# First pair of three stages as eight plain products of four weight quarters, and part 0's input normalised in two halves

## The reference

```python
a = rmsnorm(x, g_mix);  u = a @ w_in          # q, k, v, gates, o, B, C, h
h = mlstm_chunkwise(q, k, v, ...)             # four heads, plus a short convolution of C * h
x = x + concat(sigmoid(o) * headnorm(h), B * conv(C * h)) @ w_out
f = rmsnorm(x, g_ffn)
x = x + (silu(f @ w_gate) * (f @ w_up)) @ w_down
e = rmsnorm(pe @ w_ple, g_ple)
x = x + sigmoid(x @ w_pg) * e
y = rmsnorm(x, g_final)
```

## Time and profile before

| | |
|---|---|
| time, median of 3 | 2670.49 us (2669.78 to 2672.49) |
| profiled execution | 2669.71 us, of which the span is 2668.0 us |
| granted TensorE clock, mean | 0.976 |
| PE / PEld busy | 2504.5 us (94%) / 2441.3 us (92%) |
| DVE (VectorE) busy | 1477.2 us (55%) |
| ACT (ScalarE) / POOL (GpSimd) busy | 906.4 us (34%) / 1043.4 us (39%) |
| HBM traffic | 378.9 MB read, 126.3 MB written, 189 GB/s |

### The profile page before, as it was taken

One profiled execution on the slowest core, in us unless ns is written; L12 is line 12 of the kernel. 1 busy time (PEld: TensorE's weight loads), 2 busy tenths in 40 slices (PEclk: granted clock), 3 DMA queues, 4 the chain that ended last, 5 costly groups with the idle time before them and its releaser, 6 DMA issues.

```text
span 2668.0 us, 41317 instructions
## 1 busy us (share of the span) xinstructions
PE 2504.5 (94%) x15882; PEld 2441.3 (92%) x15882; DVE 1477.2 (55%) x2291; ACT 906.4 (34%) x1691; POOL 1043.4 (39%) x863
## 2 busy tenths in 40 slices
PE   4899798999999989999999999998999999999997
PEld 3899687999999989999999999998899999999997
DVE  4666787765565574466643333477347664333355
ACT  4335353433333533333421112343234432212233
POOL 3566655666676332322331222323322323222233
PEclk6999898999999999999999999999999999999998
DMA  5555644666576656566456455575557555554544
GB/s 166 194 185 189 229 167 166 221 223 227 206 252 231 209 157 212 167 228 197 158 182 206 149 169 171 175 220 186 183 177 234 181 199 167 197 193 163 174 144 158
DMA packets 292392, 507.86 MB, mean 190 GB/s; under 512 B 23892, under 2 KB 188037, under 8 KB 291687
## 3 DMA queue, kind: packets, MB, share of 16 engines
q1 hardware_dynamic: 211846, 272.28, 30.3%
q10 hardware_dynamic: 80352, 232.94, 26.8%
HBM read 378.89 MB, written 126.27 MB: 189 GB/s over the span
## 4 chain that ended last, share of the span: by engine, by line
PE 68%; DVE 9%; DMA 5%; issue 3%; POOL 2%; ACT 1%; DVEq 0%; POOLq 0%; SPq 0%; ACTq 0%
PE bank L547 22%; PE bank L549 21%; PE bank L548 21%; DMA wring<-weight_parts 3%; POOL wring L2498 2%; DMA weight_parts<-wring 1%; DVE qlo L1645 1%; PE bank L647 1%; DVE sg L2357 1%; DVE ess L2229 1%; PE bank L658 1%; DMA wraw<-w_gate 0%; PE bank L710 0%; DMA xs<-x_prompt 0%; PE bank L637 0%
## 5 line engine op out<-in xcount | busy, mean ns | idle before, releaser
L547 PE MATMUL bank<-qhi,wring 128*128 128x352 f32 (+1 forms) x3588 | 1176.9, 328 | 104.6 <-issue 20.1
L2498 POOL TENSOR_TENSOR wring<-wraw,wring 128x512 fp32r<-128x512 f32 x528 | 769.7, 1467 | 1278.5 <-ACT wring L1179 1275.9
L549 PE MATMUL bank<-qhi,wring 128*128 128x352 f32 (+1 forms) x3588 | 1159.1, 323 | 0.0
L548 PE MATMUL bank<-qlo,wring 128*128 128x352 f32 (+1 forms) x3588 | 1158.0, 323 | 0.0
L547 PEld LDWEIGHTS bank<-qhi,wring 128*128 128x128 f32 x3588 | 685.9, 191 | 132.8 <-issue 115.2
L548 PEld LDWEIGHTS bank<-qlo,wring 128*128 128x128 f32 x3588 | 685.7, 191 | 0.0
L549 PEld LDWEIGHTS bank<-qhi,wring 128*128 128x128 f32 x3588 | 683.6, 191 | 0.0
L1179 ACT ACTIVATE wring<-wraw 128x512 fp32r<-128x512 f32 x528 | 329.4, 628 | 755.0 <-PE bank L549 593.9
L547 PE MATMUL bank<-hid,wring 128*128 128x352 f32 (+1 forms) x1056 | 340.7, 323 | 11.8 <-DVE wide L2316 7.1
L549 PE MATMUL bank<-hid,wring 128*128 128x352 f32 (+1 forms) x1056 | 339.2, 321 | 0.0
L548 PE MATMUL bank<-hid,wring 128*128 128x352 f32 (+1 forms) x1056 | 338.2, 320 | 0.0
(11 more groups left out here) (305 smaller groups left out, 2441.7 us busy)
## 6 DMA issues: line engine op xcount, KB each, us to landing
wring<-weight_parts ACTq DMA_DIRECT2D x428, 512.0 KB, 4.5
weight_parts<-wring SPq DMA_DIRECT2D x206, 512.0 KB, 3.8
wraw<-w_down SPq DMA_DIRECT2D x33, 1024.0 KB, 7.1
wraw<-w_in SPq DMA_DIRECT2D x12, 1024.0 KB, 6.9
wraw<-w_in SPq DMA_DIRECT2D x48, 256.0 KB, 4.4
wraw<-w_gate SPq DMA_DIRECT2D x11, 1024.0 KB, 6.5
wraw<-w_up SPq DMA_DIRECT2D x11, 1024.0 KB, 6.2
wraw<-w_gate SPq DMA_DIRECT2D x44, 256.0 KB, 3.5
```

What stands on the lines that cost most here:

```text
L547: nc.tensor.matmul(o, hi, mh, start=begins, stop=False, skip_group_check=True)
L548: nc.tensor.matmul(o, hi, ml, start=False, stop=False, skip_group_check=True)
L549: return nc.tensor.matmul(o, lo, mh, start=False, stop=ends, skip_group_check=True)
L2498: nc.gpsimd.tensor_tensor(wlo[e % RING][:, :].rearrange(v, k=k), w.src, whi[e % RING][:, :].rearrange(v, k=k), ALU.subtract).then_inc(lo_d ...
```

## The change

It does four things.

- **Plain pairs.** `in` 0, `out` 0 and `gate` 0 no longer use the seven-product scheme. Their four weight quarters are each multiplied twice, in the order A11·B11, A21·B11, A12·B21, A22·B21, A11·B12, A21·B12, A12·B22, A22·B22, and two products add up in one of four banks. No weight sums are made, kept or loaded for these pairs, and all three parts load 1 MB raw. B12 becomes an operand of its own (number 7, in the slot of operand 6). `in` corners are copied out by ScalarE, `gate` corners by ScalarE with Silu, `out` corners added by VectorE. `gates(q)` takes four groups instead of five. The duos are gone: `out` 1 is a pair in five banks, `up` 0 a pair in three.
- **Order of operands.** T1, T2 and the rest are made during the plain pair; in parts 0 and 1 the normalising for the next part begins at product 12 of `pg` instead of 16, and T3 and T4 move from the end of `pg` into the next `in` stage.
- **Part 0's head.** Squares, roots, spreading and normalising go by halves (three tiles each); `R` is no longer normalised in place but into `wide`; stores of x move from ScalarE's queue to SP's; gains are loaded as 40 rows of 512 bytes and transposed on TensorE; ScalarE starts with a dummy Square as soon as `epst` is set; `AHEAD` work is spread among the steps.
- **Residual roots.** Column sums behind k == 4, the two spreads behind k == 7 and k == 8. The outputs of the part before (`y_gained`) move from products 6, 10, ... 26 to 7, 11, 15, 19, 23, 26 of `in`.

```diff
+PLAIN_PAIRS = {("in", 0): (0, 1, 2, 6), ("out", 0): (0, 1, 2, 3), ("gate", 0): (0, 1, 2, 6)}
+PLAIN_ENTRIES = ("A11", "A21", "A12", "A22")
+PLAIN_PRODUCTS = (("a", 0, 0, 0), ("b", 1, 0, 1), ("P2", 2, 1, 0), ("P4", 3, 1, 1),
+                  ("c", 0, B12, 2), ("d", 1, B12, 3), ("P3", 2, 2, 2), ("P5", 3, 2, 3))
+PLAIN_AHEADS = (0, 5, 6, 7)
...
-                for b, terms in enumerate((((0, 0), (1, 1)), ((0, 0), (0, 4), (1, 2)))):
+                for b, terms in enumerate((((0, 0), (1, 1)), ((0, B12), (1, 2)))):
...
-                    if k == 6:
+                    if k == 4:
                         pe.wait_ge(res_sum, 8 * (q.n + 1))
                         column_sums(("res", q.n), q, 5, ss)
-                    if k == 9:
-                        pe.wait_ge(res_root, 2 * (q.n + 1))
-                        for b in range(2):
-                            spread(("res", q.n, b), q, b, 3 + b, mean_roots)
+                    if k in (7, 8):
+                        pe.wait_ge(res_root, 2 * q.n + k - 6)
+                        spread(("res", q.n, k - 7), q, k - 7, 3 + k - 7, mean_roots)
... TensorE, head of part 0 and in_after
+            for t in range(3):
+                first_features(t)
+            gain_columns()
+            x_spread(supers[0], 0)
+            first_features(3)
+            first_features(4)
+                    if not q.n and s == 0:
+                        first_features(5)
+                    if not q.n and s == 1:
+                        x_spread(q, 1)
... ScalarE, head of part 0
+            link(nc.scalar.activation(junk[:, 0:1], epst[:, 0:1], ACT.Square))
+            for t in range(3):
+                first_squares(t)
+            act.wait_ge(consts_made, 1)
+            ahead()
+            high_of(q, "in", 0)
+            first_squares(3)
+            x_evict(q, 3, X_BANKS[3][0], 0)
+            ahead()
+            first_squares(4)
+            x_evict(q, 4, X_BANKS[4][0], 0)
+            high_of(q, "in", 1)
+            first_squares(5)
+            x_evict(q, 5, X_BANKS[5][0], 0)
+            ahead()
+            ahead()
+            high_of(q, "in", B12)
+            high_of(q, "in", 2)
... ScalarE, gate 0
+            def gate_evict(q):
+                def evict(c, b, bk):
+                    if (c, b) == (0, 0):
+                        act.wait_ge(low, LOW[(q.n, "ffn", 4)])
+                    nc.scalar.activation(sl[:, c, q.blocks[b]], bank[bk][:, 0:q.N], ACT.Silu).then_inc(silu_done, 1)
... VectorE, part 0's head
+            for t in range(3):
+                for m in range(2):
+                    x_evict(q, t, m)
+            gains()
             in_part(q, "B11")
+            in_part(q, "B21")
+            low_of(q, "in", 0)
... VectorE, pg of the part before
-                    for at_, part in ((16, "B11"), (17, "T1"), (18, "B21"), (19, "B22"), (20, "T2"), (23, "T3")):
+                    for at_, part in ((12, "B11"), (13, "B21"), (17, "B12"), (18, "B22"), (25, "T1"), (27, "T2")):
...
-                if q.n < 2:
-                    nxt = supers[q.n + 1]
-                    in_part(nxt, "T4")
-                    for i in (6, 3):
-                        low_of(nxt, "in", i)
                 gated_add(q, 3, 1)
                 gated_add(q, 3, 0)
... GpSimd
-                pool.wait_ge(x_sq, NTILE * (q.n + 1))
-                for a, z, n in ((0, 5, P), (5, 6, q.tiles[5][1])):
+                pool.wait_ge(x_sq, NTILE * q.n + (3, 6)[half])
+                for a, z, n in (((0, 3, P),), ((3, 5, P), (5, 6, q.tiles[5][1])))[half]:
... SP queue
             for t in range(NTILE):
                 sp.dma_start(xin[t][0:q.tiles[t][1], :], x_source(q, t)).then_inc(xin_in[t], 16)
                 if t == 2:
+                    gains_rows()
                     raw()
+            first_x_stores((0, 1, 2))
+            constants()
             raw()
-            constants()
+            first_x_stores((3, 4, 5))
```

More of the change, by code:

```diff
@@ L359, in add_pairs @@
[L359 to L364 removed]
+            turn = {n: n_sums[0] + j + 1 for j, n in enumerate(turns)}
+            n_sums[0] += 4
+            shift = [sum(1 for k in spares if k < j) for j in range(len(names))]
+            where = {n: e0 + j + shift[j] for j, n in enumerate(names)}
+            for j, n in zip((0, 1, 3, 6), turns):
+                sums_at.setdefault(e0 + j + shift[j], []).append((n, r, at_, where, turn))
@@ new lines, in add_pair @@
+        for j, n in enumerate(names):
+            if n in views:
+                add_entry(r, views[n], turn.get(n, 0), n == first)
+                if not stored and (n in turn or n == "A11"):
+                    keep_entry(of, n)
+                end[r] = n_prepared[0]
+            else:
+                n_loads[0] += 1
+                entries.append(Entry(r, None, 0, False, None, None, kept_as[(of, n)]))
+                entries[-1].loads = n_loads[0]
+            if j in spares:
+                add_spare(r, spares[j])
@@ L585, in pair, with plain_pair @@
                     after(base + j)
-            def duo(q, one, two, after):
-                for j, name in enumerate(FIRST_PRODUCTS):
-                    product(q, *one, name)
-                    after(2 * j)
-                    product(q, *two, name)
-                    after(2 * j + 1)
+            def plain_pair(q, st, i, after, base):
+                banks, stage, e = banks_of(st, i), st if st in STAGES else "ffn", n_entry[0]
+                for j, (name, n, op, corner) in enumerate(PLAIN_PRODUCTS):
+                    bk, starts = banks[corner], j in (0, 1, 4, 5)
+                    hi = whi[(e + n) % RING][:, :].rearrange("p (k n) -> p k n", k=4)
+                    lo = wlo[(e + n) % RING][:, :].rearrange("p (k n) -> p k n", k=4)
+                    entry_ready(e + n)
+                    operand_ready(q, stage, op)
+                    if starts:
+                        take(bk)
+                    for k in range(4):
+                        last = three(bank[bk][:, 0:q.N], hi[:, k, :], lo[:, k, :], qhi[:, slot(op), k, 0:q.N],
+                                     qlo[:, slot(op), k, 0:q.N], starts and k == 0, not starts and k == 3)
+                    multiplied((q.n, st, i, name), bk, last)
+                    operand_end[(q.n, stage, op)] = entry_end[e + n] = n_prod[0]
+                    if j < 7:
+                        after(base + j)
+                n_entry[0] += 4
             def gates(q):
@@ L951, in _ @@
-                for p in range(1 if DUO_FFN else 0, FFP):
+                plain_pair(q, "gate", 0, ffn_after(q), 0)
+                pair(q, "up", 0, ffn_after(q), 7)
+                for p in range(1, FFP):
                     pair(q, "gate", p, ffn_after(q), 14 * p)
@@ L1547, in _ @@
-                for p in range(1 if DUO_FFN else 0, FFP):
+                high_of(q, "ffn", B12)
+                plain_pair(q, "gate", 0, gate_evict(q), first_gate_after(q), 0)
+                pair(q, "up", 0, None, up_after(q, 0), 0)
+                for p in range(1, FFP):
                     pair(q, "gate", p, sl[:, 0, q.blocks[0]], gate_after(q, p), 0, ACT.Silu)
@@ L2633, in pair, with plain_pair @@
                     after(base + j)
+            def plain_pair(after):
+                for j in range(8):
+                    if j in PLAIN_AHEADS:
+                        ahead()
+                    if j < 7:
+                        after(j)
             def nothing(s):
```

745 lines of the change are left out of this document (331 added, 414 removed).

## The result

| | before | after |
|---|---|---|
| time, median of 5 | 2670.49 us (2667.13 to 2672.49) | 2685.83 us (2679.52 to 2688.12) |
| span of the profiled execution | 2668.0 us | 2684.1 us |
| ratio | | 1.0054, 95% interval 1.0039 to 1.0070 |

The changed kernel is half a per cent slower. Forecast were 2606 us and a range of 2585 to 2650: the forecast was wrong in sign, and by 80 us.

What follows compares the result with a forecast made beforehand. PE, busy 94% of the span, was taken as the bound; +11.4 - 28.4 - 17.0 - 12.4 - 17.2 - 2.6 - 0.5 + 2.0 = -64.7 us against 2669.7 gave 2605.0, forecast as 2606, range 2585 to 2650.

Steps and rivals of the forecast that it cites:

- The extra work: Plain pairs of out and gate, three parts: 72 more matmuls, +11.4 us, all on PE's path; in costs nothing.
- Head of part 0: Start of part 0, worked by halves: pair 1 of in starts at 53.2 instead of 81.6 us, saving 28.4.
- Rival 2: Head's halves don't run apart, so it saves 13 instead of 28.4 us: 2620 us; chance 12%.
- Gates wait for their second weight entry: Last step of part 0's head: ScalarE prepares the entry by 45.5 us, then four groups take 7.6 us.
- `pg` into `in`: Both part changes: earlier normalising, T3 and T4 leaving the end of pg give -10.2 and -7.0 us.
- y outputs: y_gained in in, one product before PE wants its banks: +1 us in each of parts 1 and 2.
- Entries of `out` and `gate`, part 0: Fewer weight sums on VectorE: -17.0 us at out, 6 remaining; -12.4 at gate, 16 remaining.
- Entries in parts 1 and 2: Out and gate entries: -2.6 us together at out, -0.5 at gate; bounds +8 to -6 for all four.
- rival 3: PE waits at plain pairs of parts 1 and 2, 8.8 us at four entries: slower, 2688 us; chance 6%.
- Rival 1: VectorE stays the bound at the entries and only the head gains: 2655 us; chance 17%.
- The rule on the port: VectorE and GpSimd share ports, the loser blocks: qlo 2.72 instead of 1.62 us beside GpSimd's weight entries.
- The three signs of a wrong forecast: Head saves under 20 us; PE waits over 3 us on GpSimd's operand-2 qlo per plain pair; VectorE's qlo mean above 2.

Runs made afterwards that it cites:

- g2: f3 with T4 subtracted one product sooner, ahead of the low half of T2 on VectorE: 2642.8 us, ratio 0.9905.
- h2: g2 with gate_bias ahead of the low half of T3 on VectorE: 2633.3 us, ratio 0.9873.
- e3: The changed kernel with GpSimd's clear_parts behind product 8 of in instead of 4: 2677.9 us, ratio 1.0035.
- f3: f2 with GpSimd's clear_parts after product 8 instead of 4, as in e3: 2652.9 us, ratio 0.9950.
- f4: f3 with five gate groups and ScalarE's high half of T3 ahead of its two weight conversions: 2651.8 us, ratio 0.9941.
- f1: The changed kernel with the y tiles put back toward their old places on VectorE and gate_logs after product 11 instead of 10: 2674.9 us, ratio 1.0026.
- f2: f1 with pair 1's product P4 in bank 0 instead of bank 7: 2660.7 us, ratio 0.9976.
- g1: f3 with the low half of operand 2 at the out and gate entries made by VectorE instead of GpSimd: 2660.8 us, ratio 0.9961.
- e1_bank: The changed kernel with pair 1's last product of in in bank 0 instead of bank 7: 2685.6 us, ratio 1.0071.
- e4_all_three: The changed kernel with the edits of e1_bank and e3 and five gate groups together: 2675.2 us, ratio 1.0033.
- i1: f4 with T4 sooner as in g2 and gate_bias ahead of T3's low half as in h2: 2638.9 us, ratio 0.9892.

## Why the prediction was wrong

**The extra work** was right: PE has the 72 matmuls more, and the steps of the `out` and `gate` entries in parts 1 and 2, once T4 comes sooner (g2, h2), are +0.7 to +2.4 us each, around the product of 1.9.

**Head of part 0.** Its steps held until the gates. The changed kernel's PE timeline of the head:

```profile
10.91 0.91 PE L667 MATMUL bank<-ident,x_roots 128*128 128x128 f32 x6 [0.21 <-POOL x_roots L2530]
...
17.86 0.63 PE L546 MATMUL bank<-qhi,wring 128*128 128x352 f32 x1 [2.01 <-issue]
...
25.23 1.29 PE L667 MATMUL bank<-ident,x_roots 128*128 128x32 f32 x8 [0.92 <-POOL x_roots L2530]
26.46 0.43 PE L546 MATMUL bank<-qhi,wring 128*128 128x352 f32 x1
```

The first product starts at 17.86 (18.8 forecast), the second spread is done as the third product starts, at 26.46 (28.5 and 29), and the eighth ends at 43.97 (43). Rival 2 is out. The step that failed is the last one, "Gates wait for their second weight entry, which ScalarE prepares ...: 45.5". They began at 52.14, after 8.17 us, and the first of them ran at the slow clock. I had asked only when ScalarE prepares the entry (45.64 us, so that time was right), not what stands behind that: GpSimd's part of the entry, with 3.35 us of clearing ahead of it that waits for a low half of VectorE, and the bank that ScalarE has to copy out first. So pair 1 starts at 61.3 instead of 53.2. The clearing ended last, but the 8 us don't hang on it alone: without it (e3, f3) pair 1 starts at 61.95 and 61.96, because the copy of bank 6 ends next. T4 sooner (g2) brings 59.28, h2 58.39. The last 5 us of this miss stay open.

**`pg` into `in`.** T3 and T4 no longer stand at the end of `pg`, and the first product of `in` comes 4.6 and 3.3 us sooner against the last pair of `pg`. PE's wait on `gated_add` (L2359 before, L2382 after) fell from 2.4 to 1.0 us. But the wait on VectorE's combining of the last pair only moved: from 3.1 and 2.9 us ahead of the last product of `pg` to 1.7 and 1.6 there and 3.6 and 3.5 ahead of the second product of `in`. From 911 to 955 us of the changed kernel:

```profile
PE bank L546 <- DVE sg L1712: 5.3, 2, 3.6
PE bank L656 <- DVE wide L2382: 1.0, 1, 1.0
```

The larger part was lost at the gates, to GpSimd's clearing and the late T4: the forecast was -10.2 and -7.0, measured were -2.0 and +1.9; without the clearing (e3) they are -4.5 and -2.7, with T4 sooner as well (g2) -6.2 and -4.2. I had said "the plain pair wants T1 to T4 only for pair 1, 22.8 us later" and did not follow T3 to where it lands: it shares its slot with B12, so it can't be written before the gates end, at which time pair 1 begins. Room of 22.8 us was room of zero. By itself that is worth little over 1 us a part (f4); it counts through what stands behind T3 on VectorE. With the order mended (h2) the two stretches give -7.1 and -3.0, at or inside the bounds of the forecast.

**y outputs.** This is the step that failed most: "+1 us in each of parts 1 and 2". I measured the move by one product, and left out what it was moved past: the low half of T3, `gate_bias` and, for the second tile, `gate_logs`, each with a wait of its own. It was the question that costing a moved step should have asked. Pair 1 lost 12.6 and 12.4 us, and 5.3 in part 0, where there are no y tiles and bank and gate chain alone are at work. f1 and f2 show it: with the order of the y tiles and the bank put back, the step of pair 1 falls by 9.5 and 9.3 us. The whole kernel gains 25 us between the profiled spans (2684.1 and 2658.8), 21 by the ratios. `gate_bias` ahead of the low half of T3 (h2) takes another 1.2 and 1.1 us, and 4.0 in part 0.

The Trainium skill, "PSUM — Partial Sum Buffer", Engine vs sequencer instructions, says of the queues of ScalarE, VectorE and GpSimd that they are strictly first in, first out; the rows of 955 to 1005 us agree: VectorE spent 13.87 us ahead of T3 while the first tile of y, whose root GpSimd had made by 958.80, stood behind it, and ScalarE 13.37 us ahead of T3's high half.

**Entries of `out` and `gate`, part 0.** Forecast -15.1 and -10.5, measured -5.0 and -1.1, and -7.2 and -3.8 in h2. The mechanism was there (the waits of the earlier trace rows on L1755 are gone), the size was not. I let 6 and 16 us remain by counting VectorE's work; what remains, 15.2 and 25.5, is waits of other classes and the slow clock beside them.

At `out` the gain lies ahead of its first product, 8.4 us, where the wait of 6.1 us on L1705 went. From there to the embedding the changed kernel takes 3.4 us more, the extra product included: its longest wait comes at 309.25 us. PE's waits from 266 to 312 us:

```profile
PE bank L546 <- DVE t L1715: 4.3, 1, 4.3
PE bank L546 <- DVE u L1715: 2.9, 1, 2.9
...
```

VectorE was busy without a wait from 302.39 to 309.10 us, and 3.37 us of that are sums of the residual's squares (L2184, L2187), which now stand ahead of the combining that PE waits for; my count of VectorE's work at this entry left them out. That they set the wait is read from the order, not tried.

At `gate`, the changed kernel's waits of PE from 343 to 439 us:

```profile
PE bank L546 <- POOL wring L2508: 4.6, 1, 4.6
PE bank L546 <- DVE u L1739: 4.4, 2, 3.8
PE bank L546 <- DVE wide L2339: 3.9, 1, 3.9
PE bank L546 <- POOL qlo L2522: 2.6, 1, 2.6
...
```

The 3.8 is the one of the earlier trace rows that I had said would stay. The 4.6 on GpSimd is 0.7 in h2_bias_first, whose entry is 2.7 us shorter; the other three stay (5.1, 4.5 and 2.6). What sets them was not tried. This part of the miss, some 10 us at each of the two entries, is located but its cause stays open.

**Entries in parts 1 and 2.** Forecast +4.5 in all with the extra products, measured +13.7, within the bound (8 + 7.6) but at its far end. The new wait of P3 on GpSimd was named but taken, with that of T3, at half a us; it was 1.9 us at the `gate` entry of part 1, and 1.7 to 1.9 are left in g2 and h2. The T4 chain was not seen; g2 shows it to be worth 10 us over all parts, half of that in `in`.

**The rivals.** The time fell beside rival 3's 2688, but not by rival 3: its four entries lost 13.7 us together and not 35, and the loss lay in pair 1 of `in`. Rival 1 had the right kind of cause. VectorE isn't full at pair 1 of `in`, though: its queue waits. The rule on the port holds where the two engines meet. f3_outputs_bank0_late at the entry of `out`, VectorE and GpSimd, and then g1_low2_vector's VectorE, where GpSimd makes no low half:

```profile
1167.76 4.65 DVE L1869 TENSOR_TENSOR wide<-wide 128x1408 f32<-128x1408 f32 x1
```

```profile
1167.68 3.24 POOL L2523 TENSOR_TENSOR qlo<-wide,qhi 128x1408 fp32r<-128x1408 f32 x1 [1.88 <-ACT qhi L1227]
```

```profile
1168.10 1.62 DVE L1874 TENSOR_TENSOR wide<-wide 128x1408 f32<-128x1408 f32 x1
```

T1 takes 1.62 us alone. With GpSimd's 3.24 beside it, begun 0.08 us earlier, it takes 4.65 and ends 1.49 us after GpSimd's, as though it had begun only then. The Trainium skill, "SBUF — State Buffer", Terms, has this rule, and the trace agrees. But over all of VectorE's low halves the mean didn't rise (1785 ns before, 1773 after; by source both ways, from `qraw` 1823 to 1782, from `mixq` 1605 to 1925). And g1, which takes GpSimd's low half away at these entries, gains 1 us at each `out` entry of parts 1 and 2 and loses 3 at each `gate` entry. So the rule doesn't carry the loss, as rival 1 would have it.

The three signs of a wrong forecast hardly spoke. The head saved 20.3 us, just over the 20. PE's wait on GpSimd's low half was over 3 us in one plain pair alone (`in` of part 0, 3.3). And VectorE's low halves, from 8 us ahead of a plain pair to the next pair, took 1.55 to 1.81 us in the mean in parts 1 and 2; only `in` and `gate` of part 0 were above 2 (2.11 and 2.16; 1.62 and 2.05 before). None of them looked at pair 1 of `in`, where most was lost.

## What to carry to other kernels

A step that is moved in a hand-written order is to be priced by the waits that it now stands behind on its engine, and by who wants its result, not by how far it moved: here one place in VectorE's queue, with a bank that was given back late as well, was worth 9 us in each of two parts. An operand that gets room in time needs room in memory as well: look up which buffer it shares and who reads that last. And where two waits stand one behind the other, taking away one can show nothing (e1_bank, e4_all_three); look how long the others grew before a suspect is dropped, and take them away together. A wait that ended last also isn't worth its length: e3 took 4.7 us of PE's wait away in the head, and pair 1 came no sooner.

## What the runs showed of the hardware that was not expected

- The clock can make a stall dearer than its length, and the same stall doesn't always do it. In f1_outputs_first the gate group behind a wait of 4.0 us (955.9 us) and the product behind one of 5.0 us (984.3 us) each took 3.36 us from the first start to the last, at a granted 0.50 (1.2 GHz). In the changed kernel's head the product behind 3.3 us (39.9 us) took 1.83 at a granted 1.00 (2.4 GHz); in e3_clear_late the same product behind the same 3.3 us (41.15 us) took 3.37 at 0.50. Behind waits of 1.4 us in f2 (985.4 us) and 1.8 us in f3 (1256.0 us) it was 1.85 and 1.82 at 1.00, but 3.1 behind one of 1.9 us in i1 (1247.9 us). Which level follows a given wait can't be told from these rows.
- A low half on GpSimd holds VectorE up until it ends, where the two meet: the stretched instruction was T1 in f3 (4.65 us, 1.62 alone) and T4 in g2 (4.62), each ending 1.49 us after GpSimd's. Putting a more urgent step beside it costs 3 us of that step, and still paid in g2.
- Loads issued from ScalarE's queue are as late as the operand work ahead of them. At the `gate` entry of part 1, counted from its first product, two weight loads were issued after 16.98 us in f3, 18.73 in g1 and 14.89 in g2, each 0.06 us behind the start of T4's high half; the order on VectorE is the only difference between f3 and g2.
